# Mixture-of-experts stage with experts in order of load: 64 or 32 slots each, one ring of 18 weight slots, gate and up weights as one moving operand

## What is computed

```python
g_logits = xt @ w_rg + b_rg;  g_sel = top 1 of 4 groups
e_in = the 8 expert logits of that group;  top_l, top_i = top 2
wts = softmax(top_l) * softmax(g_logits)[g_sel];  eid = g_sel * 8 + top_i
# for each of 512 (token, expert) assignments:
y = (silu(x @ w1[e]) * (x @ w3[e])) @ w2[e]        # w1, w3: 1024 x 256, w2: 256 x 1024, 32 experts
h = h + sum over the token's two experts of weight * y
```

## Time and profile before

| | us |
|---|---|
| median of 3 runs | 532.96 (532.93 to 534.94) |
| the profiled execution's own time | 533.22 |
| its span, first to last instruction | 531.3 |
| PE busy | 501.2 (94%) |
| DVE busy | 297.6 (56%) |
| ACT busy | 160.6 (30%) |
| DMA, mean over the span | 265 GB/s, 141.02 MB |

### The profile page before, as it was taken

One profiled execution on the slowest core, in us unless ns is written; L12 is line 12 of the kernel. 1 busy time (PEld: TensorE's weight loads), 2 busy tenths in 40 slices (PEclk: granted clock), 3 DMA queues, 4 the chain that ended last, 5 costly groups with the idle time before them and its releaser, 6 DMA issues.

```text
span 531.3 us, 8835 instructions
## 1 busy us (share of the span) xinstructions
PE 501.2 (94%) x3475; PEld 377.5 (71%) x3475; DVE 297.6 (56%) x594; ACT 160.6 (30%) x286; POOL 5.8 (1%) x15
## 2 busy tenths in 40 slices
PE   3999999999998999999599999999999999999992
PEld 3999987979997998987475565655656566565641
DVE  3588657777795465653793454444445344445424
ACT  6482644364343354552601101011020101102023
POOL 2100000000000000000000000000000000000000
PEclk9999999999999999999889999999999999999998
DMA  8875459636344495466939999949999999978502
GB/s 299 222 225 159 137 161 389 263 100 199 101 151 146 150 378 185 154 196 237 388 114 387 422 419 417 384 162 353 426 363 425 386 396 421 368 336 316 199 1 81
DMA packets 53586, 141.02 MB, mean 265 GB/s; under 512 B 8395, under 2 KB 39474, under 8 KB 41266
## 3 DMA queue, kind: packets, MB, share of 16 engines
q1 hardware_dynamic: 53266, 140.50, 70.5%
q10 hardware_dynamic: 288, 0.07, 0.1%
HBM read 139.51 MB, written 1.05 MB: 265 GB/s over the span
## 4 chain that ended last, share of the span: by engine, by line
PE 87%; DMA 5%; DVE 3%; ACT 2%; issue 1%; SPq 0%; DVEq 0%; ACTq 0%
PE bank L1575 22%; PE bank L1601 11%; PE bank L1270 8%; PE bank L1271 7%; PE bank L1272 7%; PE bank L1475 5%; PE bank L1537 4%; DMA expert_slots<-in_w_branch 4%; PE bank L1614 3%; PE bank L1538 3%; PE bank L1256 3%; PE bank L1615 3%; PE bank L1329 2%; DMA expert_slots<-in_w_in 1%; PE bank L1493 1%; PE bank L1491 1%
## 5 line engine op out<-in xcount | busy, mean ns | idle before, releaser
L1270 PE MATMUL bank<-act_hi,w_high 128*128 128x256 f32 x384 | 111.9, 291 | 1.5 <-DVE act_lo L766 1.0
L1272 PE MATMUL bank<-act_lo,w_high 128*128 128x256 f32 x384 | 107.9, 281 | 0.0
L1271 PE MATMUL bank<-act_hi,w_low 128*128 128x256 f32 x384 | 107.9, 281 | 0.0
L759 DVE TENSOR_TENSOR w_low<-expert_slots,w_high 128x1024 fp32r<-128x1024 f32 (+4 forms) x63 | 73.0, 1171 | 55.3 <-ACT w_high L551 55.3
L551 ACT ACTIVATE w_high<-expert_slots 128x1024 fp32r<-128x1024 f32 (+4 forms) x63 | 63.2, 1020 | 82.6 <-DMA expert_slots<-in_w_branch 53.4
L1270 PEld LDWEIGHTS bank<-act_hi,w_high 128*128 128x128 f32 x384 | 72.8, 190 | 3.9 <-DVE w_low L759 2.1
L1575 PE MATMUL bank<-expert_slots,merged_t 128*64 128x256 f32 x640 | 73.3, 382 | 0.0
L1271 PEld LDWEIGHTS bank<-act_hi,w_low 128*128 128x128 f32 x384 | 72.4, 189 | 0.6 <-issue 0.2
L1272 PEld LDWEIGHTS bank<-act_lo,w_high 128*128 128x128 f32 x384 | 72.4, 189 | 0.0
L1575 PEld LDWEIGHTS bank<-expert_slots,merged_t 128*64 128x64 f32 x640 | 44.6, 137 | 24.8 <-issue 3.1
L1601 PE MATMUL bank<-expert_slots,scratch 128*64 128x512 f32 x256 | 61.6, 604 | 0.0
(11 more groups left out here) (229 smaller groups left out, 661.5 us busy)
## 6 DMA issues: line engine op xcount, KB each, us to landing
expert_slots<-in_w_exp_down SPq DMA_DIRECT2D x32, 1024.0 KB, 7.1
expert_slots<-in_w_exp_up SPq DMA_DIRECT2D x24, 1024.0 KB, 8.6
expert_slots<-in_w_gate SPq DMA_DIRECT2D x16, 1024.0 KB, 5.6
expert_slots<-in_w_exp_gate SPq DMA_DIRECT2D x16, 1024.0 KB, 13.9
expert_slots<-in_w_in SPq DMA_DIRECT2D x8, 1024.0 KB, 6.3
scratch<-in_w_exp_up SPq DMA_DIRECT2D x8, 1024.0 KB, 10.2
scratch<-in_w_exp_gate SPq DMA_DIRECT2D x8, 1024.0 KB, 13.2
apart<-in_w_exp_gate SPq DMA_DIRECT2D x8, 1024.0 KB, 8.2
```

The costliest lines, as they stand in the source:

```text
L759: ins = V.tensor_tensor(part_slice(WL, q, where), raw, f32(part_slice(WH, q, where)), ALU.subtract)
L1270: mm(dst, wh, xh, start=first, stop=False)
L1271: mm(dst, wl, xh, start=False, stop=False)
L1272: return mm(dst, wh, xl, start=False, stop=last)
```

## The change

- The experts are sorted on the chip. Positions 0 to 7 hold experts 0 to 7 as they are (`STATIC`); positions 8 to 31 hold the other 24, the fullest first. Positions 0 to 15 have 64 places, positions 16 to 31 have 32. Steps 0 to 3 serve four positions of 64 places each; steps 4 and 5 serve eight positions of 32 places, in column tiles of 32. There are 6 steps and 12 groups (two per step). The expert numbers of positions 8 to 31 reach SP through a list in SBUF (`LIST`), loaded into a register for each position.
- A gate and an up matrix lie next to each other, and one matmul of 512 moving columns covers both (`wide`). So `hidden(n, pair)` is one run of PE's, for pair 1 cut in two halves by k.
- The 96 weight matrices are loads 0 to 95 in one order (`LOADS`): for each two positions gate, up, gate, up, down, down. Load i goes to slot i mod 18. SP issues them in this order; load i waits until load i - 18 has been used: a gate or up matrix of group g by `hid_ps` reaching g + 1, a down matrix by `y_ps` reaching 2g + 2 (both halves of `down` of that group). Load 17 alone comes late: its slot holds the scratch of the sorting.
- DVE gets new work: `expert_order` before step 0 (in the place of `overflow_list`), `destinations` and a longer `overflow_list` between its steps 0 and 1; and from step 2 on the selection is built from each token's two places (`place`), ten instructions instead of four. `hidden(n, 0)` on DVE now stands ahead of the additions of the step before.
- In the mixer the gate and the branch weights have DMAs, buffers and semaphores of their own (`load_branch`), the gate load no longer waits for branch matmuls, and the early expert loads go out one per unit, at units 12 to 17 and 24 to 26.

The core of the diff:

```diff
+STEP_SLOTS = 256
+STATIC = 8
+WIDE = 16
+CAP_WIDE, CAP_NARROW = 64, 32
+STEPS = 6
+GROUPS = 2 * STEPS
+RING = 18
...
-APART_AT = NIN + 12
+APART_AT = NIN + 14
...
+        def tiles(n, pair):
+
+            if n < 4:
+                return [(4 * n + 2 * pair + e, CAP_WIDE * e, CAP_WIDE) for e in range(2)]
+            return [(WIDE + 8 * (n - 4) + 4 * pair + e, CAP_NARROW * e, CAP_NARROW) for e in range(4)]
+
+        LOADS = []
+        for g in range(GROUPS):
+            at = [position for position, _, _ in tiles(g // 2, g % 2)]
+            for i in range(0, len(at), 2):
+                LOADS += [(at[i], 0, g), (at[i], 1, g), (at[i + 1], 0, g), (at[i + 1], 1, g), (at[i], 2, g), (at[i + 1], 2, g)]
...
             def load_unit(n):
                 if n >= NRAW:
-                    m = n - NRAW
-                    sp.wait_ge(s.w_lo, 2 * m + 2)
-                    if NIN <= m < NIN + NGATE:
-                        sp.wait_ge(s.branch_ps, m - NIN + 1)
-                for dst, src in unit_dmas(n):
-                    sp.dma_start(dst, src).then_inc(raw_in[n % NRAW], 16)
...
+                    sp.wait_ge(s.w_lo, 2 * (n - NRAW) + 2)
+                dst, src = unit_dma(n)
+                sp.dma_start(dst, src).then_inc(raw_in[n % NRAW], 16)
+
+            def load_branch(g):
+
+                if g >= NRAW:
+                    sp.wait_ge(s.branch_ps, g - NRAW + 1)
...
+            def freed(i):
+
+                _, kind, g = LOADS[i - RING]
                 if kind < 2:
-                    sp.wait_ge((s.gates_ps, s.hid_ps)[kind], n * 2 + 1 + pair)
+                    sp.wait_ge(s.hid_ps, g + 1)
                 else:
-                    sp.wait_ge(s.y_ps, n * 4 + 2 + 2 * pair)
...
+                    sp.wait_ge(s.y_ps, 2 * g + 2)
+
+            for i in range(RING, LOAD_OF[STATIC, 0]):
+                freed(i)
+                load_expert(i, LOADS[i][0])
+            sp.wait_ge(s.order_ready, 1)
+            expert = {}
+            for i in range(LOAD_OF[STATIC, 0], len(LOADS)):
+                if i == LOAD_OF[STATIC, 0] + 6:
+                    sp.wait_ge(s.over_ready, 1)
+                    load_expert(RING - 1, LOADS[RING - 1][0])
+                position, kind, _ = LOADS[i]
+                if kind == 0:
+                    expert[position] = sp.value_load(LIST[0:1, position:position + 1], min_val=0, max_val=NE - 1)
+                freed(i)
+                load_expert(i, expert[position])
...
+            def destinations():
+
+                olink(V.tensor_scalar(BASE, POS, float(WIDE), None, ALU.min))
+                olink(V.tensor_tensor(BASE, BASE, POS, ALU.add))
...
+            def place(n, part, place):
+
+                after(dve, s.wselt_ps, n * 2)
+                after(dve, s.gather_ps, n * 4)
+                slot = tab("iota")[:, 0:STEP_SLOTS]
+                for t in range(TT):
+                    V.tensor_scalar(SEL[:, t, :], slot, place(0, t), None, ALU.is_equal).then_inc(s.sel_part, 1)
+                    V.tensor_scalar(WSEL[:, t, :], slot, place(0, t), WGT[:, 0, t:t + 1], ALU.is_equal, ALU.mult)\
+                        .then_inc(s.wsel_part, 1)
+                    if t:
+                        after(dve, s.wsel_ready, n * 2 + 1)
+                    V.tensor_scalar(WSEL2, slot, place(1, t), WGT[:, 1, t:t + 1], ALU.is_equal, ALU.mult).then_inc(s.wsel_part, 1)
+                    after(dve, s.sel_part, part * 2 + t + 1)
+                    V.scalar_tensor_tensor(SEL[:, t, :], slot, place(1, t), f32(SEL[:, t, :]), ALU.is_equal, ALU.add)\
+                        .then_inc(s.sel_chain, 1)
+                    after(dve, s.wsel_part, part * 4 + 2 * t + 2)
+                    V.tensor_tensor(WSEL[:, t, :], WSEL[:, t, :], WSEL2, ALU.add).then_inc(s.wsel_ready, 1)
...
             def step(n, select_next=None, add_previous=True):
 
+                hidden(n, 0)
                 if add_previous:
                     add_outputs(n - 1)
                 slot_weights(n, 0)
-                hidden(n, 0)
                 slot_weights(n, 1)
...
+            expert_order()
+            step(0, lambda: select_quad(1), add_previous=False)
+            destinations()
             overflow_list()
-            step(0, lambda: select_quad(1, QUAD, QUAD), add_previous=False)
-            with dve.Fori(1, NQ - 1) as i:
-                step(i, lambda: select_quad(i + 1, i * QUAD + QUAD, i * QUAD + QUAD))
-            step(NQ - 1)
-            add_outputs(NQ - 1)
...
+            for n in range(1, STEPS):
+                step(n, (lambda: select_sorted(n + 1)) if n + 1 < STEPS else None)
+            add_outputs(STEPS - 1)
...
+            def hidden(n, pair, ks=range(KD)):
+
+                if ks[0] == 0:
                     after(pe, s.hid_ready, n * 2 - 1 + pair)
-                wait_slots(n, parity, pair, kind)
+                    for position, _, _ in tiles(n, pair):
+                        arrived(position, 0)
+                        arrived(position, 1)
+                for k in ks:
+                    if pair == 0 and k % 2 == 0:
+                        pe.wait_ge(s.xe_ready, n * 8 + k + 2)
+                    for position, at, width in tiles(n, pair):
+                        x = xe[:, k, pair * P + at:pair * P + at + width]
+                        ins = mm(bank[pair][at:at + width, :], x, wide(LOAD_OF[position, 0] % RING // 2, k),
+                                 start=(k == 0), stop=(k == KD - 1), skip_group_check=True)
+                if ks[-1] == KD - 1:
+                    ins.then_inc(s.hid_ps, 1)
...
+            def step(n):
+
+                hidden(n, 0)
+                if n:
+                    scatter(n - 1)
                 select_t(n, 0)
-                hidden(n, parity, 0, 1)
+                hidden(n, 1, range(0, KD // 2))
                 select_t(n, 1)
-                hidden(n, parity, 1, 0)
+                hidden(n, 1, range(KD // 2, KD))
                 hidden_t(n, 0)
-                hidden(n, parity, 1, 1)
-                if gather_next:
-                    gather_part(n + 1, 0)
-                down(n, parity, 0, 0)
+                if n + 1 < STEPS:
+                    gather_part(n + 1, 0)
+                down(n, 0, 0)
                 hidden_t(n, 1)
...
+                down(n, 0, 1)
```

More of the change, by code:

```diff
@@ L77 @@
 _r = 0
-for _n, _c in (("ident", P), ("tri", 256), ("iota", CAP + 1), ("down", EG), ("code", 2 * ROUNDS * NQ),
+for _n, _c in (("ident", P), ("tri", 256), ("iota", STEP_SLOTS), ("down", EG),
                ("cos", T), ("sin", T), ("kcs", T), ("rep", P), ("dist", 384), ("mask", 384)):
@@ L362, in part_slice, with ring_loads, wide @@
             return part(w, q).rearrange("p (k n) -> p k n", k=k)[:, :, a:b]
[L366 to L372, removed]
+        def tiles(n, pair):
[7 more added lines that the diff above has]
+                LOADS += [(at[i], 0, g), (at[i], 1, g), (at[i + 1], 0, g), (at[i + 1], 1, g), (at[i], 2, g), (at[i + 1], 2, g)]
+        LOAD_OF = {(position, kind): i for i, (position, kind, _) in enumerate(LOADS)}
+        def ring_loads(r):
+            return len(range(r, len(LOADS), RING))
+        def wide(pair, k):
+            return WIDE_PAIRS[pair].rearrange("p a (k f) -> p a k f", k=KD)[:, :, k, :]
         def y_part(w, pair, half):
@@ L420, in _ @@
                 load_unit(n)
+                if 0 <= n - 1 - NIN < NGATE:
+                    load_branch(n - 1 - NIN)
                 if n == NRAW - 1:
@@ L1211, in step, with select_quad, select_sorted @@
                 y_low(n, 1, 1)
-            def select_quad(n, col, expert):
-                select(n, col)
-                weigh(n, expert)
-            select(0, 0)
-            totals()
+            def select_quad(n):
+                quad(n)
+                weigh_quad(n)
+            def select_sorted(n):
+                place(n, n - 2, lambda c, t: AT[:, n, c, t:t + 1])
+            quad(0)
+            counts()
             router_weights()
-            weigh(0, 0)
+            weigh_quad(0)
@@ L1646, in _ @@
                 gather_part(0, b, bank[4 + b], first=True)
[L1647 to L1654 removed]
+            pe.wait_ge(s.counts_sb, 1)
+            for n in range(STEPS):
+                step(n)
+            scatter(STEPS - 1)
+            count = pe.value_load(LIST[0:1, NE:NE + 1], min_val=0, max_val=MAX_OVER)
             with pe.If(count > 0):
                 with pe.Fori(0, count) as j:
+                    n = j + STEPS
                     for b in range(4):
[L1658 to L1660 removed]
+                        gather_part(n, b)
+                    for pair in range(2):
+                        over_hidden(n, pair, j)
+                        select_t(n, pair)
+                    for pair in range(2):
+                        hidden_t(n, pair)
+                        for half in range(2):
+                            over_down(n, pair, half, j)
+                    scatter(n)
             pe.end_ifs()
```

391 lines of the change are left out of this document (214 added, 177 removed).

## The result

The kernel with the change takes 549.14 us (median of 4 runs, 546.1 to 550.0); the kernel before, measured beside it, took 533.06. The ratio is 1.0277, with a 95% interval of [1.023, 1.0325]: 3% slower. The profiled execution took 550.0 us, with a span of 548.0. The prediction said 555.6 us.

The account below looks back on a forecast made before the run. PE bounds the kernel before; DMA becomes the bound in steps 4 and 5. Step 4 starting at 400.8, loads with two pauses, tail and clock gave 551.2, plus 2.6 for tiles 553.8 span: 555.6 us, range 541 to 568 at 0.58.

Parts of the forecast that it names:

- the middle of the sum: Steps 4 and 5: DMA pauses twice, behind loads 69 and 93; the pauses and the clock carry 42 us.
- Start of step 4: Before step 4: 395.7 before the change, less 3.7 for the mixer, plus 6.4 and 2.4, gives 400.8.
- The mixer: Mixer: PE's gaps of 2.35 and 1.30 us go, -3.7 us (bounds 0 and -4).
- The wait for the lists: Step 1: PE queues behind DVE's `destinations` and `overflow_list`, a 12.4 us chain; +6.4 us (bounds 3 and 9).
- `place`: Steps 1 to 3: DVE's ten selection operations delay PE by 0.8 us a step, +2.4 us.
- `hidden(4, 1)` waits for load 69: Step 4: PE, done with all else at 412.2, stands still for 15 us until load 69 lands at 427.5.
- The clock: Steps 4 and 5: half clock after each long PE pause costs 2.8 us, three times on the chain.
- Tiles of 32 columns: Steps 4 and 5: four tiles side by side lose little, +2.6 us (bounds 0 and +25.6).
- Two by two: Rival for steps 4 and 5: tiles of 32 columns gain nothing over pairs, 579 us; chance 0.22.
- From the end of the last `down` to the end of the span: End of the kernel: 13.95 us as before, plus 2.8 for the clock.
- The rival in which the stream does not pause: Steps 4 and 5: loads 70 and 94 do not hold back DMA, span 509.4, 511 us; chance 0.14.
- The rate of 424 GB/s: Expert loads: DMA's rate from the window where all DMAs are busy, 2.47 us for each 1 MiB load.

Follow-up runs that it names:

- The kernel with the early `down`: Changed kernel with `down` of pair 0 ahead of `hidden(n, 1)` on PE in steps 4 and 5; 518.7 us, ratio 0.9698.
- the mixer alone: The kernel before with only the change's mixer part (`load_branch`, own semaphores, expert loads spread out); 530.01 us, ratio 0.992.
- the version with the lists in one piece: Changed kernel with 26 of DVE's 43 list operations moved into step 0, 14 of them in one piece; 544.95 us, ratio 1.0191.
- The filled version: Changed kernel with 58, 62, 62 and 24 matmuls of unread results in PE's waits for DMA; 544.26 us, ratio 1.0177.
- the fastest kernel: Changed kernel with early `down`, filling matmuls, loads 18 to 65 in slot-release order and list operations where DVE waits; 505.22 us, ratio 0.9459.

## Why the prediction was right, and where it was not

The mechanism was the one forecast: the order of PE and SP makes the transfers pause twice, and the steps with 24 MiB have no PE work to hide them. The kernel with the early `down` shows the middle of the sum. Step by step, as predicted and as measured:

- Start of step 4: 400.8, measured 400.59. The total is right by luck: errors of its terms cancel. The mixer gave -2.1 (step 0 starts at 270.77, not 272.91) instead of -3.7; step 0 starts between 269.25 and 271.03 in the eleven profiles that have this mixer, so the 1.6 between the two may be chance, and the mixer alone gained 3.3. Step 0 took 27.3 instead of 27.9. The wait for the lists was 6.48 instead of 6.4, and DVE's chain took 12.5 (299.67 to 312.2) instead of 12.4, though the operations listed for it in the prediction add up to 11.9. `place` cost nothing: steps 2 and 3 take 31.44 us each, against 31.6 before, so +2.4 was too high. In their place stood a price that I had left out: behind the wait of 6.48 the granted clock was 0.50, and the eight matmuls of `scatter` had a pitch of 0.43 us instead of 0.23, 1.6 in all. I knew the clock's price and took it only for the longer waits. In the version with the lists in one piece the same price stood behind a wait of 1.90. The window behind the wait of 6.48:

```profile
314.00:316.00 2.00, 2.00 (x6) 1.52 (x6) 0.43 (x2) 0.00 (x0) 0.00 (x0) 0.50 0.89 352
```

- `hidden(4, 1)` waits for load 69 until 427.5: measured 428.59, after a wait of 16.6 (15 predicted).
- Load 70 issued at 445.4: measured 445.06. The hole is there, 2 GB/s from 428 to 445.
- `hidden(5, 0)` at 478: measured 477.50. `hidden(5, 1)` at 507.7: measured 508.35. Load 94 issued at 522.7: measured 522.71. Load 95 landed at 530.7: measured 530.16.
- The clock: 2.8 us for each of three waits on the chain, 8.4. Measured 5.81 - 3.58, 5.19 - 3.58 and 6.22 - 3.74: 2.2, 1.6 and 2.5, together 6.3. The right mechanism, taken too near to its long end. The filled version shows that it is the clock: where the filling left a wait of only 1.8 us, the run took 3.64.
- Tiles of 32 columns: +2.6 predicted, 0 measured. The run of 64 instructions took 7.05 us, that of 32 wide ones 7.02. Two by two, at 579 us, falls with the same row. The Trainium skill ("TensorE: Matmul & The Clock Gate", Measured speedup vs the span model) has 2.38 times for three such tiles. This trace has no run of three; with four it does not bear out a loss of that size: 64 instructions at 0.43 us each on the full array would be 27.5, and they took 7.05, 3.9 times less.
- From the end of the last `down` to the end of the span: 13.95 predicted from before, 11.6 measured (536.38 to 548.0). Up to the norm's last product both kernels take 8.5 us (517.35 to 525.88, 536.38 to 544.92); the difference is in the store behind it, where SP's wait for `out_y` is 2.3 us instead of 4.6. It is 2.3 in every version of the changed kernel and 3.6 in the kernel before with the new mixer. Why stays open.

The errors of the tiles, the clock and the tail, 2.6 + 2.1 + 2.3 us, less 1.2 that came late elsewhere, make the 5.8 between the predicted span of 553.8 and the measured 548.0. One wait of PE was not in my text, the 6.5 us for load 71 ahead of `down(4, 1)`; it lies inside the landing of loads 70 and 71, which the sum has from SP's side, and cost nothing more.

The rival in which the stream does not pause gave 509.4 as span; the kernel with early `down`, which makes it true, has 517.5. Its sum put only the last `down` behind the last landing, with its end at 495.5. But `hidden(5, 1)` itself starts only at 488.62, behind load 93, and it, its transposes and two `down` runs take PE to 505.9. That is 10.4 later, less the 2.3 of the tail.

The rate of 424 GB/s held: 428, 421 and 420 in the slices between the holes. I had weighed it against the 358 GB/s of the Trainium skill's page on DMA. Another of its pages, "HBM Reference", Specifications (TRN2), says that this is the share of a core whose neighbour streams too, and that a core alone reaches about 425. This trace, of a kernel on one core, agrees with that, so the 358 GB/s was the wrong one of the two figures to weigh.

## What to carry to other kernels

When a ring of buffers is refilled in a fixed order, write down for each load which operation frees its buffer, and ask whether that operation itself stands behind a wait for a later load of the same stream; where it does, the stream pauses for one landing plus all the work between, and here moving the freeing operation forward in its engine's order gained 30.4 us. Packing work for one engine more tightly gains only as far as the other's stream can follow, so work out bytes per step and not only in total. Small operations that are moved into an engine's gaps belong ahead of the instruction that waits there; directly behind it they delay exactly what the other engine is waiting for, and here a wait of 1.90 us cost another 1.6 in half clock.

## What the runs showed of the hardware

- Four column tiles of 32 in float32 run side by side at full rate: 64 instructions of 512 moving columns in 7.05 us, 32 in two tiles of 64 in 7.02.
- Behind PE's waits for DMA of 2.21 to 17.9 us, in the versions here, the granted clock's half level (1.2 GHz) made the run that followed 1.5 to 3.0 us longer: 1.7 us behind a wait of 2.21 (8.80 instead of 7.05), 1.7 behind one of 17.92 (8.73). So the price did not grow with the length of the wait.
- Of four shorter waits three had no such price. Behind 1.77, 1.78 and 1.89 us the runs took 3.64, 3.64 and 7.11 us, full speed; behind a wait of 1.90 us in the version with the lists in one piece the granted clock was 0.50 for some 3 us, and it cost 1.6.
- Transfers of 1 MiB each, issued by one queue, held 415 to 423 GB/s in the fastest kernel from 284 to 475 us while PE, DVE and ACT worked, but for the window from 400 to 420 with 404.
